# A two-layer decoder trunk on one core: seven matmuls without use behind each of the three inner norms given up

## The reference, cut to what matters

```python
for l in range(DEPTH):                       # DEPTH = 2
    h = rmsnorm(x, norm1_g[l]) * (1 + sc1) + sh1
    z = h @ w_cat                            # the large input product
    ...                                      # three mixers, merged
    x = x + gt1 * (merged @ w_out[l])
    h2 = rmsnorm(x, norm2_g[l]) * (1 + sc2) + sh2
    x = x + gt2 * conv_gated_mlp(h2, ...)    # the up and down products
return rmsnorm(x, final_g)
```

## Time and profile before

| | us |
|---|---|
| runs of the kernel before | 1173.0, 1180.38, 1188.28 |
| their median | 1180.38 |
| the profiled execution, own time | 1178.63 |
| its span, first to last instruction | 1176.8 |
| mean granted TensorE clock over the span | 0.985 |
| TensorE busy | 1136.1 |
| VectorE busy | 843.5 |
| ScalarE busy | 567.5 |

### The profile page before, as it was taken

One profiled execution on the slowest core, in us unless ns is written; L12 is line 12 of the kernel. 1 busy time (PEld: TensorE's weight loads), 2 busy tenths in 40 slices (PEclk: granted clock), 3 DMA queues, 4 the chain that ended last, 5 costly groups with the idle time before them and its releaser, 6 DMA issues.

```text
span 1176.8 us, 24134 instructions
## 1 busy us (share of the span) xinstructions
PE 1136.1 (97%) x10120; PEld 1031.2 (88%) x10120; DVE 843.5 (72%) x1246; ACT 567.5 (48%) x867; POOL 78.3 (7%) x120
## 2 busy tenths in 40 slices
PE   6999999999999999999999899999999999999997
PEld 6889877887779999999988698778887899999996
DVE  5468989477476798986635689876765767888763
ACT  2236547621175666653332374675124556666433
POOL 0000010002101000001110000000030020000001
PEclk9799999999999999999999899999999999999999
DMA  9856463334055466658744445441521455545550
GB/s 378 302 190 242 151 213 146 142 143 146 17 190 205 164 221 226 234 213 290 274 151 181 175 151 199 173 162 71 200 90 72 180 214 180 178 178 182 217 210 36
DMA packets 40951, 214.34 MB, mean 182 GB/s; under 512 B 7680, under 2 KB 8064, under 8 KB 21536
## 3 DMA queue, kind: packets, MB, share of 16 engines
q1 hardware_dynamic: 29344, 171.13, 39.8%
q0 software_dynamic: 11520, 41.95, 10.4%
HBM read 212.01 MB, written 1.05 MB: 181 GB/s over the span
## 4 chain that ended last, share of the span: by engine, by line
PE 83%; DVE 11%; issue 3%; DMA 2%; ACT 1%; POOL 0%; SPq 0%; DVEq 0%; ACTq 0%
PE ps L1603 13%; PE ps L1604 13%; PE ps L1605 13%; PE ps L1616 9%; PE ps L1778 6%; PE ps L1776 6%; PE ps L1782 6%; PE ps L1880 4%; DVE RLO L1105 2%; DMA mring<-wmod_dram 2%; PE ps L1572 2%; DVE macc L1001 2%; PE ps L1582 1%; PE ps L1563 1%; PE ps L2055 1%
## 5 line engine op out<-in xcount | busy, mean ns | idle before, releaser
L1473 DVE TENSOR_TENSOR WLO<-ring,WH 128x1024 fp32r<-128x1024 f32 x144 | 176.0, 1229 | 89.8 <-ACT WH L859 89.8
L859 ACT ACTIVATE WH<-ring 128x1024 fp32r<-128x1024 f32 x144 | 151.6, 1058 | 183.0 <-PE ps L1605 167.9
L1603 PE MATMUL ps<-HH,WH 128*128 128x256 f32 x736 | 208.3, 283 | 0.0
L1604 PE MATMUL ps<-HL,WH 128*128 128x256 f32 x736 | 208.3, 283 | 0.0
L1605 PE MATMUL ps<-HH,WLO 128*128 128x256 f32 x736 | 208.3, 283 | 0.0
L1603 PEld LDWEIGHTS ps<-HH,WH 128*128 128x128 f32 x736 | 141.3, 192 | 0.0
L1604 PEld LDWEIGHTS ps<-HL,WH 128*128 128x128 f32 x736 | 141.3, 192 | 0.0
L1605 PEld LDWEIGHTS ps<-HH,WLO 128*128 128x128 f32 x736 | 141.3, 192 | 0.0
L1603 PE MATMUL ps<-GH,WH 128*128 128x256 f32 x384 | 109.6, 285 | 0.0
L1604 PE MATMUL ps<-GL,WH 128*128 128x256 f32 x384 | 109.4, 285 | 0.0
L1605 PE MATMUL ps<-GH,WLO 128*128 128x256 f32 x384 | 109.3, 285 | 0.0
(11 more groups left out here) (387 smaller groups left out, 2482.5 us busy)
## 6 DMA issues: line engine op xcount, KB each, us to landing
ring<-wmain_dram SPq DMA_DIRECT2D x150, 1024.0 KB, 4.9
mring<-wmod_dram POOLq DMA_DIRECT2D x80, 512.0 KB, 5.0
G<-wmod_dram SPq DMA_DIRECT2D x3, 1024.0 KB, 7.3
R<-wmod_dram SPq DMA_DIRECT2D x3, 1024.0 KB, 15.4
TK<-wmod_dram SPq DMA_DIRECT2D x2, 1024.0 KB, 20.5
X<-x_t_dram SPq DMA_DIRECT2D x1, 1024.0 KB, 9.3
SW<-small_dram SPq DMA_DIRECT2D x2, 512.0 KB, 13.7
y_dram<-H SPq DMA_DIRECT2D x4, 256.0 KB, 2.2
```

What stands on the lines that cost most here:

```text
L859: A(WH[:, n % 2, part], ring[:, b, part], ACT.Copy).then_inc(hi_ready, 1)
L1473: V.tensor_tensor(WLO[:, n % 2, part], ring[:, b, part], WH[:, n % 2, part].bitcast(F32), ALU.subtract).then_inc(lo_ready, 1)
L1603: MM(out, w_high[:, at], high, start=start, stop=False, skip_group_check=True)
L1604: MM(out, w_high[:, at], low, start=False, stop=False, skip_group_check=True)
```

## The change

The three calls behind the inner norms are taken out, and nothing else. The calls in the preamble stay.

```diff
                 out(2, 0, KT)
                 out(3, 0, KT)
-                keep_clock(7, 6, C[:, 0:S])
 
                 g0 = PAIRS * l + UP
...
                 ones_sum(2 * l + 2)
-                if l == 0:
-                    keep_clock(7, 6, C[:, 0:S])
```

## The result

The changed kernel takes 1185.32 us (median of 20 runs, 1180.12 to 1192.68). The kernel before, run on the same chips in the same rounds, takes 1180.77 (20 runs, 1173.0 to 1188.47). The ratio is 1.005 with a 95% interval of [1.0031, 1.0068]: 3.7 to 8.0 us slower, within 2%. So the 7.9 us between the two spans are not the effect, and the traces must be read place by place.

What follows compares the result with a forecast made beforehand. TensorE was taken as the bound, busy 1136.1 of 1176.8 us. Direct gain 0, clock falls 0.9 + 1.7 + 0.9 = 3.5 us, giving 1182.1 from the profiled execution or 1183.9 from the median; 1183.0 taken, range 1173 to 1192.

Steps and rivals of the forecast that it cites:

- No direct gain, as nothing removed lay on the path: At all three norms the useless matmuls end before ScalarE's first tile, so removing them gains 0 us directly.
- The clock falls at all three: Behind each of the three inner norms, idle gaps of 3.68 us make the granted clock fall once.
- Between 1.82 us without and 4.51 with a fall, nearest to the `mod_sum`: The 3.68 us gaps lie between waits that held and lost the clock, nearest the `mod_sum`'s 3.3 us, with a fall.
- The price, 0.9 + 1.7 + 0.9: Loss in us per fall: second norm of layer 0, first norm of layer 1, second norm of layer 1.
- where the low stretch begins: Behind a second norm, unknown start between the first pair and the end of the tiles' pace; 0.9 us taken.
- my bounds: Second norm: a 3.4 us low stretch costs 0.4 us from the first pair, 1.7 from when the pace ends.
- the stretch that I had named: The low clock should begin between one microsecond ahead of a norm's first useful matmul and three behind it.
- Sum 3.5 us: The three norms' falls together cost 3.5 us, with ends of 0 and 12.7.
- The range of 1173 to 1192: Forecast range for the whole kernel in us, holding also the spread of the earlier runs, 1173.0 to 1188.28.
- That the clock doesn't fall: Rival at the three norms: no fall, or one too brief to cost; time stays 1179 to 1180; chance 0.19.
- The value path's 10.2 us: Rival: low stretches at the norms as long as behind layer 1's value path; up to +12.7, 1191 us; chance 0.10.
- the preamble's 17: Rival: some 17 us at half speed at each norm, as in the preamble; +25.5 us, 1204; chance 0.03.

Runs made afterwards that it cites:

- The kernel with fourteen: Fourteen useless matmuls in place of seven behind each of the three inner norms of the kernel before; 1188.65 us, ratio 1.007.
- the thin matmuls: Thirteen one-column matmuls in place of the seven 256-column ones behind each inner norm of the kernel before; 1185.77 us, ratio 1.0053.
- the changed kernel with fills: Changed kernel plus useless matmuls in the value path's wait and ahead of layer 0's `mod_sum`; 1179.46 us, ratio 1.001 to the kernel before.

## Why the prediction was right, point by point

*No direct gain, as nothing removed lay on the path: right.* The wait grew from 0.49 to 3.5 us and the norm stayed at 3.48. The kernel with fourteen shows the other side: the moment the useless matmuls outlast the norm, they cost their surplus.

*The clock falls at all three: right*, and that the falls are the cause is shown from three sides: the thin matmuls keep the instruction stream and lose the clock and the time; the kernels that give up one place or two fall at these norms only; and with three useless matmuls the first norm of layer 1 had idle time and no fall, and lost nothing.

*Between 1.82 us without and 4.51 with a fall, nearest to the `mod_sum`: right in its outcome, but its lower end is not firm.* The same wait at line 1776 that held the clock in the earlier trace rows was followed by a fall in the kernel with fourteen:

```profile
748.88 0.47 PE L1776 MATMUL ps<-WC,HG 128*128 128x512 f32 x1 [1.83 <-DVE RLO L1219]
...
750.10:753.50 3.40, 3.40 (x16) 2.64 (x15) 1.93 (x2) 0.00 (x0) 0.00 (x0) 0.50 0.43 161
```

There the wait is 1.83 us and not 1.82. Waits of 1.92 (thin) and 2.30 us (the changed kernel with fills) at this place were followed by a fall as well, those of 1.2 to 1.75 us in seven other profiles were not. In layer 0, at about 165 us, a fall followed waits of 2.04, 2.20, 2.37 and 2.80 us, and none followed 2.29 and 2.53, nor five shorter ones. So from 1.8 to 2.5 us both outcomes occur in these profiles, and the idle time alone does not settle which. At the norms, 1.35 us had no fall in three, 2.22 had two in three, 3.5 had nine in nine. The gaps of the change lie above the open stretch; which part of what happens in a gap decides, its length or the little work around it, no run separates.

*The price, 0.9 + 1.7 + 0.9: right to a few tenths.* Measured at the places: 1.14, 1.59, 0.80 in the changed kernel. Over all profiled places with a fall, a second norm cost 0.41 to 1.14 (ten cases, mean 0.77) and the first 1.59 to 1.69 (four). What I had left open, where the low stretch begins, decides as my bounds said: behind a second norm it cost 0.41 and 0.45 where it began with the first useful matmul (378.2 against 378.24 with thin ones, 955.2 against 955.09 with three), and 0.92 where it began 1.3 us later (with fills). The low stretch was 3.4 us at 13 of the 14 places. The exception is the second norm of layer 0 in the changed kernel: it was 6.8 us, and began 1.8 us ahead of the first useful matmul, outside the stretch that I had named; as it lay partly over idle and paced work it cost only 1.14. That this is near 0.9 is luck.

*Sum 3.5 us.* Measured 3.7 to 8.0 by the ratio, 4.6 by the medians. The range of 1173 to 1192 would have held no change as well, so what speaks for the forecast is the ratio's interval and the three places, and not that the time lies in the range. The local sum is 3.5, so 0.2 to 4.5 us are not found at the three norms. The mean time at the lower clock rose from 35.9 us (the 28 runs) to 51.9, 16.0 more, where the three places of the profile account for 3.4 + 3.4 + 6.8 = 13.6, and three usual ones for 10.2. The kernel with thin matmuls has 16.0 more too, and that without the calls behind the second norms 12.5 more for two falls. So more time at the lower clock was added than falls at the norms explain, by some 6 us in each of these three; but the kernel with fourteen has 6.8 more without any fall at a norm, and that without the first call 4.0 for its one fall. Whether the change brings falls elsewhere, or this is chance between sets of runs, stays open. The mis-sized term, if there is one, is this: I counted no fall outside the three places.

*The rivals.* That the clock doesn't fall is refuted. The value path's 10.2 us and the preamble's 17 did not occur at a norm in any profile; the longest was 6.8.

## What to carry to other kernels

Here matmuls without use were free while they ended before the release of the next useful one, and what they bought is the clock of the dense work behind the gap: 0.4 to 1.7 us for each gap of 3.7 us. Look for the gap in TensorE's waits, size the filler to end just short of the release, use wide matmuls (256 columns here), and look for stretches where the engine is nominally busy with one-column matmuls too. A gap that nobody fills can be worth as much as those already filled: here the wait for the value path and the one at a `mod_sum` gave 5.8 us together in the mean. Judge a filler by the mean clock of many runs, as in a single execution the clock may fall or hold at the same place.

## What the runs showed that I had not expected

Most of the scatter of the kernel before from run to run goes with the clock. Over the 80 of its runs beside these experiments, time and mean granted clock are correlated at -0.92, and 0.001 less clock goes with 1.07 us more time. For comparison, 0.001 of mean clock is 2.4 us at the lower level, which would cost dense work 1.2. The runs reach from 0.980 to 0.990. The profiles show where: in the preamble, the same in all these kernels, the clock falls at about 25 us for 17.1 us in some and at about 30 for 6.8 in others, and falls at 92, 163 to 169, 661, 750 or 796 to 804 us are there in some and not in others. What decides it from run to run is not shown.

The changed kernel lies on the same line: its mean clock, 0.9781, predicts its mean time, 1185.65, within 1.3 us. The kernel with fourteen is the only one far off it, by +5.6 us, as it should be: it alone adds work to the path, 4.75 us by its profile.

Thirteen one-column matmuls filled 2.96 us of the profile's TensorE time in front of a norm's tile, and the clock fell behind them as behind an empty gap, three times out of three. The engine's busy share does not show such a gap.
